# One hybrid decoder layer on one core: sample gate and output-weight copies moved between the gate sigmoids, one-hot tables shared out over three engines, and the last LayerNorm's statistics partly on ScalarE

## What is computed

```python
proj = x @ w_in                        # u, v, xs
y_a = gelu(u) * spatial_gate(layer_norm(gelu(v)))
y_b, h = s5_mixer(xs)                  # state space scan, then
#   y = gelu(y);  z = y * sigmoid(einsum(y, w_glu) + b_glu)
x = layer_norm(ALPHA * x + concat(y_a, y_b) @ w_out)
scores = sigmoid(x @ w_router)         # 16 experts, top 2 within one group of 4
out = sum_e comb[:, e] * (silu(x @ w_gate[e]) * (x @ w_up[e])) @ w_down[e]
x = layer_norm(ALPHA * x + out)        # the last LayerNorm: mean, variance, rsqrt, gain, shift
```

## Time and profile before

| | |
|---|---|
| median of 3 runs | 1360.35 us (1359.79 to 1361.69) |
| profiled execution: its time, its span | 1360.65 us, 1359.0 us |
| busy: PE, DVE | 1196.5 us (88%), 895.2 us (66%) |
| busy: POOL, ACT | 475.1 us (35%), 458.8 us (34%) |
| end of A: barrier before the output projection | about 516 us |
| B: routing done to first tokens turned | 765 to 799 us |
| C: last LayerNorm | 1298 us to the end |

### The profile page before, as it was taken

The page is one execution under the profiler, slowest core; times in us unless marked ns, Lnnn a source line. Parts: engine busy times, 40 slices in busy tenths (PEclk is TensorE's granted clock), DMA queues, the critical chain, the costliest instruction groups (busy, mean ns, idle before and its releaser), DMA issues. The chain is left out here.

```text
span 1359.0 us, 22638 instructions
## 1 busy us (share of the span) xinstructions
PE 1196.5 (88%) x6653; PEld 955.5 (70%) x6654; DVE 895.2 (66%) x1980; ACT 458.8 (34%) x679; POOL 475.1 (35%) x553
## 2 busy tenths in 40 slices
PE   7999999799879777999999259999999999999910
PEld 6997999778767544888888257767767767767600
DVE  3452876468877564466667667777777777777586
ACT  4221110110012451222221125556556555556433
POOL 3008850200110014322222023545545545445267
PEclk9999999899989988999999579999999999999965
DMA  8555342564154322433332546787977777644484
GB/s 258 173 198 161 142 125 65 155 228 175 64 165 147 111 87 67 153 111 112 119 119 97 224 163 195 214 245 225 253 201 227 210 211 216 145 98 98 117 309 174
DMA packets 112874, 222.84 MB, mean 164 GB/s; under 512 B 51304, under 2 KB 68280, under 8 KB 103568
## 3 DMA queue, kind: packets, MB, share of 16 engines
q1 hardware_dynamic: 96368, 164.86, 36.0%
q0 software_dynamic: 15408, 55.12, 17.3%
q10 hardware_dynamic: 1040, 2.10, 0.4%
HBM read 144.34 MB, written 77.58 MB: 163 GB/s over the span
## 5 line engine op out<-in xcount | busy, mean ns | idle before, releaser
L2030 DVE TENSOR_TENSOR wgu<-w_raw,wgu (+1 forms) x192 | 226.0, 1219 | 52.5 <-ACT wgu L2117 52.4
L2211 PE MATMUL p_gu<-wgu,xg_high 128*128 x768 | 254.2, 412 | 4.5 <-DVE xg_low L2023 4.5
L2117 ACT CAST wgu<-w_raw (+1 forms) x192 | 187.1, 1050 | 19.3 <-SPq L1845 16.6
L2211 PEld LDWEIGHTS p_gu<-wgu,xg_high 128*128 128x128 f32 x768 | 145.1, 190 | 59.0 <-issue 31.3
L2234 PE MATMUL p_d<-wd,ht 128*128 x384 | 174.9, 598 | 1.8 <-DVE ht L2044 1.0
L2211 PE MATMUL p_gu<-wgu,xg_low 128*128 x384 | 151.8, 395 | 0.0
L2234 PEld LDWEIGHTS p_d<-wd,ht 128*128 128x128 f32 x384 | 69.0, 189 | 71.5 <-issue 71.2
L1710 PE MATMUL p_out<-w_out_high,mixt_high 128*128 128x512 f32 (+1 forms) x272 | 108.2, 398 | 12.4 <-POOL mixt_low L1487 12.4
L1710 PE MATMUL p_out<-w_out_high,mixt_low 128*128 128x512 f32 (+1 forms) x272 | 106.6, 392 | 0.0
L1710 PE MATMUL p_out<-w_out_low,mixt_high 128*128 128x512 f32 (+1 forms) x272 | 106.4, 391 | 0.0
L1914 POOL TENSOR_TENSOR spare_e<-nothing 128x1 f32<-128x1 f32 x48 | 9.2, 192 | 233.2 <-DVE yo L2050 233.2
(11 more groups left out here) (434 smaller groups left out, 2677.6 us busy)
## 6 DMA issues: line engine op xcount, KB each, us to landing
w_raw<-in_w_gate SPq DMA_DIRECT2D x16, 1024.0 KB, 4.8
w_raw<-in_w_up SPq DMA_DIRECT2D x16, 1024.0 KB, 7.8
wd<-in_w_down SPq DMA_DIRECT2D x16, 1024.0 KB, 4.9
acc_rows<-ax SPq DMA_DIRECT2D x18, 512.0 KB, 5.7
xin<-in_x_prompt SPq DMA_DIRECT2D x16, 512.0 KB, 6.3
sq<-sq_mats SPq DMA_DIRECT2D x16, 512.0 KB
z<-in_x_prompt SPq DMA_DIRECT2D x16, 512.0 KB, 4.1
x_rows<-x SPq DMA_DIRECT2D x16, 512.0 KB, 4.9
```

The lines of the kernel that those rows point to most:

```text
L2030: low = tt(wgu[:, slot, 1, at], raw[:, slot, at], wgu[:, slot, 0, at].bitcast(F32), ALU.subtract)
L2117: nc.scalar.copy(wgu[:, slot, 0, at], raw[:, slot, at]).then_inc(hi_set, 1)
L2211: mm = t.matmul(pg[b][:, :, :], x[:, b, k, :], w[h][:, k], start=(k == 0 and x is xh and h == 0), stop=(k == KD - 1 and x is xl))
```

## The change

In A, PE and ACT take the sample's gate earlier: the GELU stands behind gate 7 instead of gate 15, PE turns it after `state_rows(2)` and multiplies it after `state_rows(5)`, and the copies of `w_out` stand one by one between the gates. POOL makes the low parts of slices 0 to 4, DVE those of 5 to 7. In B, DVE writes both plain one-hot tables `hot` first and then both `rowhot`; POOL makes three of the four products `tilehot`, ACT the fourth in 17 instructions; `g_idx` moves ahead of the small tables and has its own signal (`lists_set` 1; `s_idx` gives 2). In C, the string `KINDS` says for each place n of the order who does the tile: N as before; S: ACT sums the tile (a copy with an accumulated output into `sum2`), scales the sum to minus the mean (`low2`) and accumulates the squares of the centred values (`ssq2`), DVE only makes the variance of it; U: as S, and DVE instead of ACT and POOL multiplies by the power and adds the shift.

```diff
@@ stage A, POOL, ACT, DVE, PE
-                for k in range(0, KD, 2):
+                for k in range(5):
                     gp.wait_ge(wo_high, k + 1)
...
-                for n in range(4 * FT):
+                def gate(n):
...
+                for n in range(8):
+                    gate(n)
                 act.wait_ge(ys_set, 1)
                 nc.scalar.activation(mixs[:, 1, :], ys_row[:, 0:WA], ACT.Gelu_apprx_tanh).then_inc(ys_gelu, 1)
                 act.wait_ge(w_out_in, 16)
+                gate(8)
                 w_high(0)
+                gate(9)
+                gate(10)
                 w_high(1)
+                gate(11)
                 act.wait_ge(ys_turned, 1)
                 nc.scalar.copy(yts[:, 0], pst[1][:, 0, 0:FT * NS].rearrange("p (f s) -> p f s", s=NS)).then_inc(ys_copied, 1)
+                gate(12)
                 w_high(2)
+                gate(13)
                 act.wait_ge(gs_prod, 1)
...
-                for k in range(3, KD):
+                gate(14)
+                w_high(3)
+                gate(15)
+                for k in range(4, KD):
                     w_high(k)
...
-                for k in range(1, KD, 2):
+                for k in range(5, KD):
                     dve.wait_ge(wo_high, k + 1)
...
                 for n in range(8):
                     glu(7 + n)
                     state_rows(n)
+                    if n == 2:
+                        sample_gate_in()
+                    if n == 5:
+                        sample_gate()
                 glu(15)
@@ stage B, POOL, DVE, ACT, PE
+                for k in range(2):
+                    gp.wait_ge(hot_set, k + 1)
+                    gp.tensor_tensor(tilehot[:, k, :, 0, :], hot[:, k], id1[:].unsqueeze(2).broadcast_to(st_), ALU.mult).then_inc(ids_put, 1)
+                gp.tensor_tensor(tilehot[:, 1, :, 1, :], hot[:, 1], gate_k[:, 1, :].unsqueeze(2).broadcast_to(st_), ALU.mult).then_inc(ids_put, 1)
                 gp.wait_ge(lists_set, 1)
...
+                dve.wait_ge(list_prod, 1)
+                ch(ts(lst[:], p_ls[:, 0, :], -1.0, None, ALU.add))
+                ch(ts(pad[:], lst[:], 0.0, None, ALU.max))
+                v.tensor_copy(g_idx[:], pad[:]).then_inc(lists_set, 1)
                 ch(ts(tab[:, 3, :], tfl[:], 1.0, None, ALU.add))
...
+                act.wait_ge(hot_set, 1)
+                for c in range(TILES):
+                    nc.scalar.mul(tilehot[:, 0, c, 1, :], hot[:, 0, c, :], gate_k[:, 0, c:c + 1]).then_inc(gates_put, 1)
...
-                    pe.wait_ge(hot_set, k + 1)
+                    pe.wait_ge(row_set, k + 1)
+                    pe.wait_ge(ids_put, (1, 3)[k])
+                    if k == 0:
+                        pe.wait_ge(gates_put, TILES)
@@ stage C, POOL, DVE, ACT
+            KINDS = "NSNUNSNNSUNSNNSUN"
...
+                    if KINDS[n] != "N":
+                        dve.wait_ge(ssq_set, n + 1 - KINDS[:n + 1].count("N"))
+                        ts(var2[0:r, n:n + 1], ssq2[0:r, n:n + 1], 1.0 / D, EPS, ALU.mult, ALU.add).then_inc(var_set, 1)
+                        return
...
+                    else:
+                        stt(row, row, low2[0:r, n:n + 1], g, ALU.add, ALU.mult).then_inc(centred, 1)
+                    if KINDS[n] == "U":
+                        dve.wait_ge(centred, n + 1)
+                        dve.wait_ge(rstd_set, n // 2 + 1)
+                        stt(row, row, rstd2[0:r, n:n + 1], b2_row[0:r, :], ALU.mult, ALU.add).then_inc(shifted_dve, 1)
...
+                def act_stats(n, c):
+                    if KINDS[n] == "N":
+                        return
+                    r, m = tokens(c), n + 1 - KINDS[:n + 1].count("N")
+                    act.wait_ge(acc_in[c], 16)
+                    nc.scalar.activation(junk[0:r, :], zi[0:r, c, :], ACT.Copy, accum_out=sum2[0:r, n:n + 1]).then_inc(low_set, 1)
+                    act.wait_ge(low_set, 2 * m - 1)
+                    nc.scalar.mul(low2[0:r, n:n + 1], sum2[0:r, n:n + 1], -1.0 / D).then_inc(low_set, 1)
+                    act.wait_ge(low_set, 2 * m)
+                    nc.scalar.activation(junk[0:r, :], zi[0:r, c, :], ACT.Square, bias=low2[0:r, n:n + 1],
+                                         accum_out=ssq2[0:r, n:n + 1]).then_inc(ssq_set, 1)
+                    act.wait_ge(ssq_set, m)
...
+                for n, cs in PAIRED:
+                    for k, c in enumerate(cs):
+                        act_stats(n + k, c)
+                    if n:
+                        for k in range(2):
+                            scale(n - 2 + k, ORDER[n - 2 + k])
+                scale(TILES - 1, ORDER[TILES - 1])
```

More of the change, by code:

```diff
@@ L1356, in _, with sample_gate_in, sample_gate @@
                 pe.wait_ge(fin_copied, 1)
+                def sample_gate_in():
+                    pe.wait_ge(ys_gelu, 1)
+                    for f in range(FT):
+                        mm = t.transpose(pst[1][:, 0, f * NS:(f + 1) * NS], mixs[:, 1, f * P:(f + 1) * P], ident[0:NS, 0:NS])
+                    mm.then_inc(ys_turned, 1)
+                def sample_gate():
+                    pe.wait_ge(ys_copied, 1)
+                    for f in range(FT):
+                        mm = t.matmul(pst[1][:, 0, 64 + f * NS:64 + (f + 1) * NS], wbd[:, f].rearrange("p g q -> p (g q)"),
+                                      yts[:, 0, f, :], start=True, stop=True)
+                    mm.then_inc(gs_prod, 1)
                 for n in range(8):
@@ L1795, in hybrid_step @@
             spare2 = sb("spare2", [P, 1], where=rows)
+            sum2, low2, ssq2 = (sb(n, [P, TILES], where=rows) for n in ("sum2", "low2", "ssq2"))
             half2, tab_r = sb("half2", [P, 2], where=rows), sb("tab_r", [P, 2], I32, where=rows)
@@ L1802, in hybrid_step @@
             assert pt.at <= base + 153 * KB
+            junk = sb("junk", [P, D], where=Place(nc, base + 35 * KB))
             zi = sb("zi", [P, TILES, D], where=Place(nc, base + 53 * KB + 2 * GU * 4))
@@ L1906, in add @@
                 def add(i, b, first):
-                    if not first:
+                    if first:
+                        gp.wait_ge(lists_set, 2)
+                    else:
                         gp.wait_ge(added[b], (i - b) * 8)
@@ L2003, in _ @@
                 ts(tab[:, 4, :], tix[:], 2.0, float(E), ALU.add, ALU.min).then_inc(te_set, 1)
-                dve.wait_ge(list_prod, 1)
-                ch(ts(lst[:], p_ls[:, 0, :], -1.0, None, ALU.add))
                 ch(v.tensor_copy(gates[:], p_ls[:, 1, :]))
-                ch(ts(pad[:], lst[:], 0.0, None, ALU.max))
-                ch(v.tensor_copy(g_idx[:], pad[:]))
+                dve.wait_ge(lists_set, 1)
                 ch(stt(pad[:], lst[:], 0.0, padrow[:], ALU.is_lt, ALU.mult))
@@ L2099, in _ @@
                         dve.wait_ge(g_set, 2)
+                        dve.wait_ge(row2_in, 32)
                     else:
@@ L2168, in _, with scale @@
                     nc.scalar.copy(pt_x[h].rearrange("p k n -> p (k n)"), g2_row[:, h * SUP:(h + 1) * SUP]).then_inc(g_set, 1)
-                for n, c in enumerate(ORDER):
+                def act_stats(n, c):
+                    if KINDS[n] == "N":
+                        return
+                    r, m = tokens(c), n + 1 - KINDS[:n + 1].count("N")
[7 more added lines that the diff above has]
+                    act.wait_ge(ssq_set, m)
+                def scale(n, c):
+                    if KINDS[n] == "U":
+                        return
                     r = tokens(c)
```

49 lines of the change are left out of this document (22 added, 27 removed).

## The result

The changed kernel took **1369.41 us** (median of 6 runs, 1366.84 to 1371.79), the kernel before 1361.02 (6 runs, 1359.20 to 1363.42). The ratio is 1.0052, with a 95% interval of 1.0040 to 1.0064: **7.1 us slower** (5.4 to 8.7). The forecast was slower, 1369.4, by 9.0 us. That the time was hit to 0.01 us is luck: the ratio asks for 7.1 where 9.0 were forecast, the two medians lie 8.4 apart, and the median before stood 0.7 above the one that the forecast started from. The profiled run after is the lowest of the six, 1366.84 us with a span of 1365.2, 6.2 over the span before.

A forecast was written before the change was run, and what follows sets the result against it. PE bounds the kernel, but only in the expert loop; the three changed places lie outside it, so their gains and losses count whole. From 1360.35, -0.7 - 1.3 + 11.0 = +9.0 gave 1369.4 us, range 1360.0 to 1378.5.

The forecast's parts named there:

- Part A: End of the GLU stage: 0.7 us gained, after giving half back for the clock; bounds 7.4 gained, 1.4 lost.
- The placing: End of the GLU stage: every operation placed in order ends at 514.4 against 515.8 before, a gain of 1.4 us.
- the ring of four: GLU stage: a held-up product delays ACT's next gate, that the next copy, and that POOL; such gaps add 1.6 us.
- The step on the clock: GLU stage: PE's products come more thinly and its clock may fall; half of the 1.4 us gain given back.
- Part B: Making of the expert lists: 1.3 us gained, 0.9 from POOL beginning earlier, 0.4 from the issue; bounds 2.9 gained, 1.0 lost.
- Part C: Last LayerNorm: 11.0 us lost, 9.0 to 15.8; DVE ends 14.2 later, the last scaling and shift take 3.8 more.
- the ring: Last LayerNorm: centring, two scalings, ACT statistics, centring in series; a round takes 6.65 or 9.35 us against 5.64.
- S: Last LayerNorm: time of ACT's statistics for one tile, 2.7 us, between 2.45 and 3.3; 0.8 us lost per 0.1.
- The first (exclusion spares the short products): Rival, GLU and list stages: short products run beside POOL without waiting; gains 7.4 and 1.9, total 1362.0 us; chance 0.10.
- The second (dear accumulated outputs, S of 3.3): Rival, last LayerNorm: S is 3.3 or more, 15.8 us lost there, total about 1374.2 and up; chance 0.10.
- The third (hidden ACT statistics): Rival, last LayerNorm: ACT's statistics run hidden, DVE's work falls from 48.1 to 41.2, 7 us gained, total 1351; chance 0.08.
- The fourth: Rival, all three places: short products escaping the exclusion, S at its low end and full clock cancel; 1360, no change; chance 0.06.

The follow-up runs named there:

- b_only: The change's list-making edits alone, the other two places as in the kernel before; ratio 1.0000 (0.9991 to 1.0009) against the kernel before, 0.0 us.
- a_no_pool: The change's GLU-stage edits alone, but all eight `w_out_low` on DVE and none on POOL; 0.9974 against the kernel before, 3.5 us faster.
- c_psum: The last-LayerNorm edits alone, with ACT's statistics one pair sooner and the U tiles' shift row read from PSUM; 0.9948 against the kernel before, 7.1 us faster.
- c_split: c_psum with another share of tiles, three S and six U; 0.9898 against the kernel before, 13.9 us faster.

## Why the prediction was right, and where it wasn't

**What bounds what.** Right for C: the place lies outside the expert loop, and its loss went into the time whole (+10.3 timed, 8.4 to 12.4, for a stage that is 9.45 longer). For B alone it isn't shown: `b_only`'s trace is 1.4 shorter there, its time by at most 1.2.

**Part A**, -0.7 forecast. The placing was right: 1.4 sooner at the barrier, measured 1.5 (27.6 to 26.1); gate 8 at 491.6, measured 491.61. The product that is held up does delay ACT's next gates, but by way of `h_rows` and PE's queue and not by the ring of four. The step on the clock was not borne out: the clock didn't fall while the GLU products ran. What slows the projection's start is a clock at 0.50 that both kernels have, and its length scatters. The single pair of traces has 12.48 before and 13.31 after from the first `p_out` to the first `z`, but six more kernels without the edit have up to 14.08 and a mean of 12.94, three with it 13.21: 0.3 given back, in a scatter of 1.6. The sum should have held -1.2 here. The load of ACT's table behaved as the row said and not as the page of the Trainium skill (ScalarE: Activation LUTs, What ACT_TABLE_LOAD costs), whose drain of about 1.38 us a switch would, by an estimate from that figure, have put gate 8 at 494.4: GELU starts 0.01 us behind the load and gate 8 0.02 behind the second.

**Part B**, -1.3 forecast, -1.5 by the traces (29.09 to 27.57). The total is near, its split was not. In this pair `gi` came 0.85 sooner (0.9 forecast), but over the kernels it starts 18.68 us behind the `id` product without the edit (18.18 to 18.92) and 18.15 with it (17.33 to 18.90): 0.5 sooner. The other 1.0 lies behind `gi`, where 0.4 were forecast: from `gi` to the first `p_gu` it is 10.41 without (10.06 to 10.61) and 9.42 with it (9.36 to 9.48), and the first issue took 1.13 each time instead of 2.04, or 1.69 in two. PE ended its lists 16.12 us behind the `id` product, before 15.41; forecast were 1.1 later, measured 0.7. That end scatters too, from 15.4 to 17.1 without the edit: the clock rises to 1.00 between 9.6 and 13.2 us behind the `id` product, while PE is at work on the lists. That POOL and DVE take turns was forecast and stands in the 7.47 us of the two `rowhot`, 3.8 each where over 4 was said.

**Part C**, +11.0 forecast, +9.45 measured, the ring and its places as told: DVE idle 3.82 us ahead of tile 8 and of tile 14. S was taken as 2.7 and measured 2.68 (1317.98 to 1320.65 is 2.67, 1295.63 to 1298.31 is 2.68), by errors that cancel: two instructions of 0.19 that the forecast left out, against handoffs of 0.02 to 0.03 where it had 0.1 and a readout that starts 0.09 before its sum's end. The rounds, by the ends of DVE's centrings:

| round | forecast | measured |
|---|---|---|
| the first, tiles 0 to 3 | about 0 | -0.1 |
| tiles 4,5 | +1.0 | +0.7 |
| U 3, U 9, each | +1.4 | +1.3 |
| tiles 8,9 and 14,15, each | +3.7 | +3.4 |
| tiles 10,11 | +1.0 | +0.7 |
| the last, with U 15 | +2.0 | +1.9 |
| DVE's end | +14.2 | +12.6 |
| last scaling and shift behind it | 3.8 | 3.8 |

The term that was mis-sized is the round's overhead: 0.25 for DVE's variance was in fact 0.07, since only the last of it stands ahead of the centring (1323.34 to 1323.41), and ACT took its next instruction 1.15 behind the last centring, not 1.3 (1316.83 to 1317.98). That is 0.3 in each of the four rounds of the ring (6.36 instead of 6.65, 9.05 instead of 9.35), 1.2 of the 1.55 us; the rest is 0.1 in each U tile and in the first round.

**The sum.** With the measured terms it is -1.2 - 1.5 + 9.45 = +6.7, and the timed ratio says +7.1. The forecast of 9.0 is 1.9 over that; the interval of the ratio (5.4 to 8.7) doesn't hold it.

**The rivals.** The first (exclusion spares the short products) falls by the 2.23 to 2.36 us of the gate products and by `a_no_pool`. The second (dear accumulated outputs, S of 3.3) falls by S = 2.68, though its two further instructions of 0.19 are there. The third (hidden ACT statistics) didn't happen in this order; `c_psum` and `c_split` show the stage that it described. Its own terms (8 x 1.63 off; 8 x 0.2 and 3 x 1.3 on) bring DVE's 48.1 to 40.6, not 41.2. The fourth falls with the first.

## What to carry to other kernels

Before work is moved to a second engine, draw the ring: if engine X needs Y's result for pair p, and Y's queue holds pair p's work behind something that needs X's pair p-1, every round costs the sum of both; issuing the independent half one pair sooner took 9 us out of this kernel. An idle GpSimd is no free engine here: where its elementwise work met a VectorE operation with two operands in SBUF, one of the two waited, so such work was faster left on VectorE, or with one operand moved to PSUM. Size a gain of one or two us inside the trace, between two marks around the edit and over several kernels, since the work ahead of the edit alone drifted by 2.7 us.

## What the runs showed that I had not expected

- The exclusion between POOL and DVE isn't always one operation each in turn: a DVE operation of 1.28 us took 5.99 beside POOL operations back to back, and 1.28 with one operand in PSUM. In stages A and B the turns were kept; what makes the difference isn't known.
- An accumulated output on ACT is an instruction of its own, ACTIVATION_READ_ACCUMULATOR, of 0.19 us. Two of them are in S.
- The clock's rise came 2.7 to 5.9 us behind the projection's first matmul in the 12 kernels without the extra ones, and each us of that stretch costs half a us. Its scatter alone is as large as the gains sought in A. PE's work shortly ahead of an idle stretch of 2.44 us moved the fall into the projection without shortening the slow stretch by more than 0.4 us.
